# Tile start addresses: moving tiles of the products at 64 bytes, stationary tiles at 0 or 192, modulo 256

## What is computed

```
h  = modulate(rmsnorm(x, norm1_w), shift, scale)          # (2048, 1024)
hc = modulate(rmsnorm(ctx, norm1_w), shift_c, scale_c)    # (256, 1024)
u  = h @ w_in                                             # w_in (1024, 2848); for hc only the columns of k, v and the decays
y  = concat(conformer_conv, gla, short_conv) @ w_out      # (1024, 1024)
x  = x + gate1 * y
h  = modulate(rmsnorm(x, norm2_w), shift2, scale2)
gate, idx = top_k(softmax(h @ router_w), 256)             # each of 16 experts picks 256 tokens
xs = h[idx]                                               # (16, 256, 1024)
hid = silu(xs @ w1) * (xs @ w3)                           # per expert, (1024, 1024) weights
x  = x + gate2 * scatter_add(hid @ w2 * gate)
out = rmsnorm(x, final_norm_w)
```

## The kernel before

| operands | stationary | moving | moving minus stationary, modulo 256 |
|---|---|---|---|
| input projection: `whi`/`wlo`, `h`/`hc` | 0 | 0 | 0 |
| input projection, first tile: `wa`, `h`/`hc` | 0, 128 | 0 | 0, 128 |
| output projection: `ct`, `wo` | 0 | 0 | 0 |
| expert up: `shi`/`slo`, `xt` | 0 | 32 | 32 |
| expert down: `ht`, `shi`/`slo` | 0 | 0 | 0 |
| turning: `xs`, `ident_r` | 0 | 160 | 160 |

## Time and profile before

### The profile page before, as it was taken

One profiled execution on the slowest core, in us unless ns is written; L12 is line 12 of the kernel. 1 busy time (PEld: TensorE's weight loads), 2 busy tenths in 40 slices (PEclk: granted clock), 3 DMA queues, 4 the chain that ended last, 5 costly groups with the idle time before them and its releaser, 6 DMA issues.

```text
span 2153.7 us, 35092 instructions
## 1 busy us (share of the span) xinstructions
PE 2074.7 (96%) x13569; PEld 1815.5 (84%) x13569; DVE 1369.9 (64%) x2082; ACT 996.1 (46%) x1631; POOL 277.8 (13%) x357
## 2 busy tenths in 40 slices
PE   6999999999999899997999999999999999999996
PEld 4778888888878677785899999999999999999985
DVE  3664648995994577757555656556555665656557
ACT  5923454444531445431444544445444444445455
POOL 0001000100001010020011122111221112111120
PEclk9999999999999999998999999999999999999998
DMA  7463333333427665456357666576565765657565
GB/s 258 150 248 132 109 106 99 115 118 88 125 77 237 236 208 176 145 214 257 118 204 246 215 215 211 187 264 214 193 216 195 273 198 186 217 218 253 198 233 225
DMA packets 188285, 407.95 MB, mean 189 GB/s; under 512 B 15956, under 2 KB 53396, under 8 KB 187300
## 3 DMA queue, kind: packets, MB, share of 16 engines
q1 hardware_dynamic: 162212, 318.36, 42.6%
q0 software_dynamic: 25984, 88.39, 12.6%
HBM read 329.59 MB, written 77.12 MB: 189 GB/s over the span
## 4 chain that ended last, share of the span: by engine, by line
PE 80%; DVE 10%; ACT 3%; DMA 3%; issue 2%; SPq 1%; POOL 0%; DVEq 0%; ACTq 0%; POOLq 0%
PE bh L55 11%; PE bh L57 11%; PE bh L56 11%; PE bank L55 8%; PE bank L57 8%; PE bank L56 8%; PE eby L55 5%; PE eby L57 5%; PE eby L56 5%; DVE acc L854 3%; PE ebt L2283 1%; PE bank L1031 1%; DVE over L2012 1%; PE bank L1413 1%; DVE raw L2472 1%
## 5 line engine op out<-in xcount | busy, mean ns | idle before, releaser
L55 PE MATMUL bh<-xt_hi,shi 128*128 128x256 f32 x2048 | 572.2, 279 | 3.2 <-DVE slo L2436 2.7
L56 PE MATMUL bh<-xt_lo,shi 128*128 128x256 f32 x2048 | 571.6, 279 | 0.0
L57 PE MATMUL bh<-xt_hi,slo 128*128 128x256 f32 x2048 | 571.4, 279 | 0.0
L2436 DVE TENSOR_TENSOR slo<-raw,shi 128x1024 fp32r<-128x1024 f32 x384 | 456.0, 1221 | 156.9 <-ACT shi L2345 152.4
L2345 ACT ACTIVATE shi<-raw 128x1024 fp32r<-128x1024 f32 x384 | 389.8, 1052 | 127.1 <-PE eby L57 125.5
L55 PEld LDWEIGHTS bh<-xt_hi,shi 128*128 128x128 f32 x2048 | 385.3, 188 | 4.6 <-issue 2.5
L56 PEld LDWEIGHTS bh<-xt_lo,shi 128*128 128x128 f32 x2048 | 385.4, 188 | 0.6
L57 PEld LDWEIGHTS bh<-xt_hi,slo 128*128 128x128 f32 x2048 | 385.3, 188 | 0.0
L55 PE MATMUL bank<-h_hi,whi 128*128 128x512 f32 x704 | 283.4, 403 | 0.0
L57 PE MATMUL bank<-h_hi,wlo 128*128 128x512 f32 x704 | 275.4, 391 | 0.0
L56 PE MATMUL bank<-h_lo,whi 128*128 128x512 f32 x704 | 275.4, 391 | 0.0
(11 more groups left out here) (348 smaller groups left out, 3127.6 us busy)
## 6 DMA issues: line engine op xcount, KB each, us to landing
raw<-in_exp_w_dram SPq DMA_DIRECT2D x96, 2048.0 KB, 11.0
uT<-stage POOLq DMA_DIRECT2D x72, 256.0 KB, 2.7
xb<-in_ada_w_dram SPq DMA_DIRECT2D x24, 512.0 KB, 5.6
wraw<-in_w_in_dram SPq DMA_DIRECT2D x22, 512.0 KB, 5.4
adaw<-in_ada_w_dram SPq DMA_DIRECT2D x8, 1024.0 KB, 9.7
xb<-in_x_dram SPq DMA_DIRECT2D x16, 512.0 KB, 4.2
xt<-in_x_dram POOLq DMA_DIRECT2D x16, 512.0 KB, 5.3
x2d<-xt POOLq DMA_DIRECT2D x16, 512.0 KB, 3.0
```

Source lines behind the costliest of these rows:

```text
L55: nc.tensor.matmul(out, w_hi, x_hi, start=start, stop=False)
L56: nc.tensor.matmul(out, w_hi, x_lo, start=False, stop=False)
L57: return nc.tensor.matmul(out, w_lo, x_hi, start=False, stop=stop)
L2436: nc.vector.tensor_tensor(item_dst(slo, n), item_src(n), item_dst(shi, n), ALU.subtract).then_inc(S["w_lo_ready"], 1)
```

## The change

The tiles are moved in SBUF. No instruction is added, taken away or put in another place; one wait is added on ScalarE.

```
@@ phase_project
-        gap = sb("gap", [P, 8])
+        gap = sb("gap", [P, 56])
@@
-        ssq, msq, rst = (sb(n, [P, 18]) for n in ("ssq", "msq", "rst"))
+        ssq, rst = (sb(n, [P, 18]) for n in ("ssq", "rst"))
+        msq = v.tok[:, :, :].rearrange("p e s -> p (e s)")[:, 0:18]
@@ route_stage
         v.hot_free = (S["blocks_ready"], 1)
+        v.found_free = (S["list_ready"], 1)
@@ phase_experts
-        shi = [sb(f"shi{i}", [P, D], F32R) for i in range(NR)]
-        slo = [sb(f"slo{i}", [P, D], F32R) for i in range(NR)]
+
+        def behind(shift):
+            at[0] += (shift - at[0]) % 256
+
+        shi, slo = [], []
+        for i, shift in enumerate((0, 0, 0, 0)):
+            behind(shift)
+            shi.append(sb(f"shi{i}", [P, D], F32R))
+            slo.append(sb(f"slo{i}", [P, D], F32R))
         xs_words = [sb(f"xs{i}", [P, D], F32R) for i in range(2)]
         xs = [t[:, :].bitcast(F32) for t in xs_words]
-        at[0] += 32
+        behind(64)
         xt_hi, xt_lo = sb("xt_hi", [P, KD, CAP], F32R), sb("xt_lo", [P, KD, CAP], F32R)
-        at[0] += 224
+        behind(192)
         ht_hi, ht_lo = sb("ht_hi", [P, FD, CAP], F32R), sb("ht_lo", [P, FD, CAP], F32R)
@@
-        ssq, msq, rst, nt = (sb("f_" + n, [P, NT + 2]) for n in ("ssq", "msq", "rst", "nt"))
+        small = sb("f_small", [P, 4 * (NT + 2)])
+        ssq, msq, rst, nt = (small[:, i * (NT + 2):(i + 1) * (NT + 2)] for i in range(4))
@@ scalar engine
                 for n in range(NR):
+                    if n == NR - 1:
+                        act.wait_ge(*v.found_free)
                     split(0, n)
@@ trunk_kernel
                 hsb, ps = alloc(nc, hst)
+                hsb("h_gap", [P, 16])
+                low = nc.sbuf_base
                 v.h_hi, v.h_lo = hsb("h_hi", [P, L // NB, KD, NB], F32R), hsb("h_lo", [P, L // NB, KD, NB], F32R)
```

## The result

| | before | after |
|---|---|---|
| median | 2156.1 us (4 runs) | 2169.64 us (4 runs, 2167.92 to 2173.03) |
| ratio | | 1.0064, 95% interval 1.0046 to 1.0082 |
| profiled span | 2153.7 us | 2166.2 us |

The changed kernel is 0.64% slower, 13.5 us. The forecast was 2118.5 us, and the time lies just outside its range of 2080 to 2168 us.

A forecast was written before the change was run, and what follows sets the result against it. TensorE was taken to bound the kernel; 3021 x 6.6 ns = 19.9 us plus 5760 x 3.3 ns = 19.0 us, together 38.9, took 2155.37 to 2116.5 us, and 2.0 us for the median gave 2118.5; range 2080 to 2168 us.

The forecast's parts named there:

- What bounds the kernel: Middle experts: TensorE has no idle time (68.00 of 68.00 us), so faster products shorten an expert one for one.
- The loss is a price per product and does not grow with the columns: Split products at distance 0: each loses 13.3 ns at 256 columns and 13.2 at 512, whatever its columns.
- The next 32 bytes bring as much: Going from 32 to 64 bytes gains 3.3 ns again: 6.6 ns per product from 0, 3.3 per up product.
- the counts of the prediction: Products that can gain: 5760 up, 1440 down and 1581 in the input projection, the last expert left out.
- The distance matters at all: Split products: pace depends on moving start against stationary start modulo 256; 13.3 ns lost at 0, 10.0 at 32.
- nothing depends on the start addresses: Rival, all products: the 3.3 ns come from something else and the loss stays everywhere; 2157.4 us, chance 0.11.
- 64 as bad as 0: Rival, up products: their loss returns to 13.3 ns, +19.0 us, nothing gained elsewhere; 2176.4 us, chance 0.19.
- over at 32 bytes: Rival: 32 bytes part the streams, so only the 3021 products from 0 gain, 3.3 ns each; 2147.4 us, chance 0.20.
- wholly parted rival: Rival, all split products: 64 bytes leave only 3.0 ns lost, together 71.1 us gained; 2086.3 us, chance 0.14.
- The added wait, the packing, `raw` and `wraw` at other starts: ScalarE's wait for `list_ready` in expert 0, packed small tiles, and moved copy and DMA tiles: each 0 us.
- The pace as the test: Profile after: start-to-start pace decides, not mean duration; right would be 113.4 ns up, about 220 ns projection and down.

The follow-up runs named there:

- the fastest kernel: Kernel with up products at distance 192, projection and down at 0, plus one transpose ahead of each expert's up products: 2138.19 against 2155.77 us, ratio 0.9917.
- first kernel of the series: Changed kernel with the start addresses of before, the rest of the change kept: 2155.81 against 2156.15 us, ratio 1.0001.

## Why the prediction was wrong, point by point

- *What bounds the kernel* was right: TensorE has no idle time in a middle expert, and every nanosecond of its pace came through, both ways. In the fastest kernel 1.17 us less per expert became 17.6 us in total.
- *The loss is a price per product and does not grow with the columns* failed. The 13.3 and 13.2 ns agree at distance 0 and at no other distance that was run. At 32 the loss is 20 ns for 512 columns and 10 ns for 256; at 192 it is 20 and 6.7.
- *The next 32 bytes bring as much* is the step that turned the sign. It drew a line through two of a few separate values, 120.0 and 116.67 ns. In place of -6.6 ns for the 512-column products the change brought +2.6 in the projection and +1.7 in the down products; in place of -3.3 ns for the up products, +1.03. Only the 96 context products went the forecast way, -3.3 ns. By the counts of the prediction that is 1440 x 1.7 = 2.4 us and 5760 x 1.03 = 5.9 us in the experts (measured alone: 7.7 us), and 1485 x 2.6 = 3.9 us less 0.3 in the projection (measured alone: 4.9 us).
- *The distance matters at all* was right, and is now shown rather than argued: moving only one or only the other tile gives the same paces for the 512-column and the up products. The rival that *nothing depends on the start addresses* (2157.4 us) falls with it. The rule of the Trainium skill ("TensorE: Matmul & The Clock Gate", on what happens when a matmul is issued) of two independent read ports, by which the sum would be 0, is not borne out: between distances the paces differ by up to 6.9 ns for 512 columns (227.3 and 234.2) and 6.7 ns for 256 (113.33 and 120.0), in kernels that differ in start addresses alone.
- *The rival "64 as bad as 0"* had the sign and the right reason against a slope ("two points make no curve"), but only part of the products. It was to be decided on `bh` alone, from 1.7 ns on; `bh` lost 1.03, and the 512-column products, for which it expected no loss, did the rest. Its 2176 us were too high, the range's upper end of 2168 us 1.6 us too low.
- *The rival "over at 32 bytes"* (2147.4 us) fell: the up products did not stay at 116.7 ns, and the 512-column products did not come near 223 ns at any distance.
- *The wholly parted rival* (3.0 ns lost) fell: the least loss in any run is 6.7 ns for 256 columns (113.33) and 13.3 ns for 512.
- *The added wait, the packing, `raw` and `wraw` at other starts*, each costed at 0, were right (first kernel of the series: ratio 1.0001).
- *The pace as the test* was the right thing to look at, but it was read from one expert. Expert 0 of the kernel before runs at 117.78 ns and all others at 116.67. From its first up product to its last (start us, us, what; kernel before, to be set against the first and last `bh` of the earlier trace rows, 44.68 us apart):

```profile
1040.30 0.39 PE L55 MATMUL bh<-xt_hi,shi 128*128 128x256 f32 x1 [0.55 <-DVE xt_lo L2452]
...
1085.52 0.28 PE L57 MATMUL bh<-xt_hi,slo 128*128 128x256 f32 x1
```

  It is 45.22 us, 0.54 more, of which 0.1 is the first product. Reading all the experts would have shown ahead of the change that one distance has two paces, and that a difference of 3.3 ns between two forms can be one of pattern.
- *Small misreadings:* a few rows gave 226.5 ns for the 512-column products and 120.0 for the context products, where the means are 227.3 to 227.7 and 119.5; and 1245.01 to 1313.05 is 68.04 us, not 68.06. Neither turns the sign.

What stays open: what the two streams collide in, if they do, and why a pattern is kept. The runs show that the distance and the entry choose the pattern, not what is in conflict. Each kernel's paces come from one traced execution. Distances between multiples of 32 were not tried, nor other entries for the projection, nor a tile moved by 256 bytes alone: that the count goes modulo 256 is assumed throughout and not shown.

## What to carry to other kernels

Where TensorE is the bound and runs long series of equal matmuls, read the pace from start to start for each form and each repetition of the loop: several discrete values among the repetitions mean that the same code can run at another pace, and here that was worth 4.45 ns of 118, where the shifts of the change under study were worth 1.0 to 3.3. Set start distances by a sweep for each number of columns, measured in the kernel itself and never from two points, and re-measure the entry of a series (one 0.1 us instruction ahead of it was worth 1.6 us per expert) after every change of what stands before it. The version that comes out of it, up products at 192, all others at 0, and one transpose ahead of each expert's series, takes 2138.19 us, 0.83% under the kernel before and 1.4% under the changed one.

## What the runs showed of the hardware

- The steady paces that were read are multiples of one step when averaged over a short cycle of products: 113.33, 116.67 and 120.0 ns are 34, 35 and 36 times 3.33 ns, 226.67 and 233.33 ns are 68 and 70 times, 117.78 and 228.9 ns are cycles of three products with 106 and 206 steps, 118.67 ns is a cycle of five with 178, and 118.33 ns one of eight with 284. 3.33 ns is 8 cycles of the 2.4 GHz level. The step and the multiples are worked out from the traces; what imposes them is not shown.
- A pattern once entered held for all 384 products (43.5 to 46 us), past the semaphores between items and with other engines at work.
- The start addresses of `raw`, `wraw` and the small tiles, as sources of ScalarE and VectorE and as targets of DMA, had no measurable price (ScalarE 1050 against 1052 ns a copy, VectorE 1222 against 1221, a 2 MB load 11.1 against 11.0 us).
